# A two-block transformer kernel: the order of the first mixer on four engines is rewritten

## The chip, the cores and the metric

The kernel runs on one core of a Trainium2 chip. The metric is the device time of one execution in microseconds (us). The core's engines run their own instruction streams and meet through semaphores: TensorE (PE; PEld is its weight load), VectorE (DVE), ScalarE (ACT), GpSimd (POOL) and SyncE (SP, which starts the DMAs of weights).

## The reference

Two blocks on 256 tokens of width 1024, all in float32. The change lies in the middle of the first one, its mixer; what it computes:

```python
u = rms_norm(h, ln_mix[i]) @ w_in[i]
hq, hf, hi_, hg, cq, ckv, kr = jnp.split(u, split_at, axis=-1)
log_f = jnp.log(lb + (1.0 - lb) * jax.nn.sigmoid(hf))
k_in = (1.0 - lb) * jax.nn.sigmoid(-hf)
o_hg = hgrn2_chunkwise(hq, log_f, k_in, hi_)          # 4 heads of 128
o_hg = rms_norm(o_hg, hg_out_norm[i]) * jax.nn.silu(hg)

q = rms_norm(cq, q_a_norm[i]) @ w_q_up[i]             # 4 heads, 128 + 64 rope
kv = rms_norm(ckv, kv_a_norm[i]) @ w_kv_up[i]         # keys 128, values 128
o_mla = causal_block_attention(qf, kf, v)             # softmax over 256 tokens
h = h + jnp.concatenate([o_hg, o_mla], axis=-1) @ w_out[i]
```

Before it stand a SwiGLU block (width 2816) and behind it another one, a gated embedding, and the second block: a projection with "forgetting" attention of 16 heads in four groups, and at the end a retrieval of expert rows.

## The kernel before

**Slots.** Every large product is cut into slots of 256 output columns, 2048 weights per partition. SP loads a slot into `ring`, ACT rounds it to `whi` (L947), DVE or POOL makes the rest `wlo` (L326, a split; in the mixer only POOL does it), and PE multiplies three times: high x high (L443), high x low (L444), low x high (L448); in `tokens` these are L465 to L467. A slot has two tiles, t = 0 and 1, a half slot each in `features(n)`; `tokens(n)` has two halves of 128 tokens, and frees both tiles at its end. `whi` holds two slots, so a tile can be rounded once the same half of the slot two earlier is done (`tiles_done`). The mixer's input projection has ten slots, `S_IN` to `S_IN + 9`: forget gates and queries (0 to 3), latents (4, 5), recurrence values (6, 7) and output gates (8, 9). `S_OUT` and the three behind it are the output projection.

**Levels.** The recurrence is computed in eight levels. In `level(n)` PE makes 8 blocks of scores of 128 x 128 into banks 4 and 5 (L607). In `level_read(n)` DVE copies the entries of that level through a mask (L1431); in `widen(n-1)` three DVE products in SBUF (L1445 to L1447) make the operands of level n + 1. A level can begin when the one before it is read and its operands are widened. Operands start with `qf` (L1424). A last level (L698) crosses the two halves; DVE copies it out (L1481) and PE multiplies scores with values (L706 to L708, `hg_out`).

**Latents and heads.** `latent_sums` lets PE sum squares with a stationary matrix of ones, so all partitions hold all 256 sums; ACT takes roots of all of it and DVE the reciprocal (L1456). `q_up`, `k_up`, `v_up` and `swapped` (rotation) are small products in banks 6 and 7 that ACT copies out (L1054). The heads' norm works likewise on 4 x 256 numbers: `hg_sums` (L715), root (L1083), two reciprocals (L1518, L1520).

**Attention.** `attention` makes the scores (L721, L722) and returns `values`, which turns the probabilities (L574, L578), waits for ACT's copy (L1094) and multiplies by the values (L728 to L730). DVE does `softmax` (L1494 to L1501) and `normalise` (L1508 to L1512), ACT the exponentials between them (L1088). `low_x` makes the low part of the input of the next projection (L1297). `keep_busy(n)` issues n matmuls of ones into an unused place; nobody reads them. The second block's attention uses the same functions, with two feature slots and 12 dummies between scores and values.

All orders are written out by hand, one program per engine; each engine executes its own in order.

## Time and profile before

| | us |
|---|---|
| three executions | 1594.4, 1596.62, 1597.06 (median 1596.62) |
| the profiled execution, span | 1596.27, 1594.5 |
| PE busy, DVE, ACT, POOL | 1400.5, 1004.2, 561.5, 710.3 |

Times in rows are from the start of the span. A busy PE is no proof of useful work: dummies count. A row's bracket is the idle time before it and the engine that ended it.

### The profile page before, as it was taken

How to read it: one execution, taken by the hardware profiler on the slowest of the kernel's cores; microseconds unless marked ns; L12 is line 12 of the kernel's file. 1: busy time of each engine (PE TensorE's matmuls, PEld its weight loads, DVE VectorE, ACT ScalarE, POOL GpSimd, SP SyncE). 2: the span in 40 equal slices, each digit the busy share in tenths (PEclk: the TensorE clock that was granted, in tenths of full speed). 3: DMA queues.
4: the chain of work that ended last, by engine and by line, in shares of the span. 5: the costliest groups of instructions: out<-in, count | busy, mean ns of one | idle time of the engine just before them, and what ended most of it. 6: DMA issues, size and time to landing. Idle time of an engine off the chain costs nothing.

```text
span 1594.5 us, 21201 instructions
## 1 busy us (share of the span) xinstructions
PE 1400.5 (88%) x8086; PEld 1071.4 (67%) x8086; DVE 1004.2 (63%) x1792; ACT 561.5 (35%) x947; POOL 710.3 (45%) x443
## 2 busy tenths in 40 slices
PE   8999899998999999989999998777777876877776
PEld 8999899978999998889889883333333332333322
DVE  4887464555778534552543777777777777777654
ACT  4443355424444334554343542222222222222212
POOL 3443437402343534486575485444433443444440
PEclk9999899999999999999999998999998998989998
DMA  5776673303577653243333379999999999999994
GB/s 221 264 263 229 242 251 134 106 27 116 208 263 261 213 180 107 105 135 130 106 107 112 137 289 422 422 421 421 421 421 422 421 421 422 421 422 421 422 421 187
DMA packets 59782, 427.15 MB, mean 268 GB/s; under 512 B 6640, under 2 KB 6960, under 8 KB 8624
## 3 DMA queue, kind: packets, MB, share of 16 engines
q0 software_dynamic: 36864, 268.45, 40.6%
q1 hardware_dynamic: 22176, 156.38, 27.9%
q10 hardware_dynamic: 656, 1.18, 0.2%
q8 instruction: 54, 0.88, 0.2%
q14 instruction: 32, 0.26, 0.0%
HBM read 424.93 MB, written 1.05 MB: 267 GB/s over the span
## 4 chain that ended last, share of the span: by engine, by line
PE 49%; DMA 27%; DVE 13%; ACT 4%; issue 4%; POOL 3%; DVEq 0%; SPq 0%; ACTq 0%; POOLq 0%
DMA rows_x<-in_expert_uv,arena 26%; PE ps L443 8%; PE ps L448 8%; PE ps L444 8%; PE ps L883 5%; PE ps L886 4%; PE ps L520 2%; POOL wlo L326 2%; PE ps L521 2%; PE ps L522 2%; DMA ring<-in_w 1%; DVE arena L1366 1%; DVE arena L1696 1%; ACT whi L947 1%; DVE arena L1512 1%
## 5 line engine op out<-in xcount | busy, mean ns | idle before, releaser
L326 POOL TENSOR_TENSOR wlo<-ring,whi 128x1024 fp32r<-128x1024 f32 x162 | 407.7, 2526 | 497.1 <-ACT whi L947 496.6
L443 PE MATMUL ps<-nh,whi 128*128 128x256 f32 x1440 | 364.3, 290 | 11.3 <-ACT nh L961 6.8
L947 ACT ACTIVATE whi<-ring 128x1024 fp32r<-128x1024 f32 x236 | 244.3, 1055 | 340.2 <-PE ps L448 139.4
L444 PE MATMUL ps<-nh,wlo 128*128 128x256 f32 x1440 | 355.7, 283 | 0.0
L443 PEld LDWEIGHTS ps<-nh,whi 128*128 128x128 f32 x1440 | 276.4, 192 | 17.2 <-issue 8.1
L444 PEld LDWEIGHTS ps<-nh,wlo 128*128 128x128 f32 x1440 | 276.7, 192 | 0.3
L448 PE MATMUL ps<-nl,whi 128*128 128x256 f32 x1440 | 209.2, 285 | 0.1
L448 PEld LDWEIGHTS ps<-nl,whi 128*128 128x128 f32 x1440 | 188.2, 192 | 4.9 <-DVE nl L1304 2.1
L326 DVE TENSOR_TENSOR wlo<-ring,whi 128x1024 fp32r<-128x1024 f32 x74 | 103.8, 1414 | 133.8 <-ACT whi L947 128.6
L1844 POOL DMA_INDIRECT arena<-in_expert_uv,arena x96 | 111.3, 1160 | 141.0 <-PE ps L886 129.4
L1696 DVE CUSTOM_DVE_ANT_0 arena<-arena 128x1024 f32<-128x1024 f32 x96 | 124.7, 1299 | 39.7 <-DMA arena<-in_expert_uv,arena 35.6
L1216 ACT ACTIVATE arena<-arena 128x4 f32<-128x4 f32 (+1 forms) x67 | 13.7, 205 | 348.0 <-DVEq L1698 348.0
L1844 POOL DMA_INDIRECT rows_w<-in_expert_uv,arena x64 | 65.5, 1024 | 114.8 <-PE ps L886 111.7
L1696 DVE CUSTOM_DVE_ANT_0 arena<-rows_w,arena 128x1024 f32<-128x1024 f32 x64 | 78.3, 1224 | 49.2 <-DMA rows_w<-in_expert_uv,arena 48.7
L520 PE MATMUL ps<-gh,whi 128*128 128x256 f32 x352 | 103.8, 295 | 6.2 <-DVE wlo L326 4.5
L883 PE MATMUL ps<-rows_w,silu 128*128 128x512 f32 x96 | 63.0, 744 | 51.7 <-ACT silu L1223 51.7
L1366 DVE SCALAR_TENSOR_TENSOR arena<-arena,vec 128x256 f32<-128x256 f32 x168 | 102.4, 609 | 5.9
L521 PE MATMUL ps<-gh,wlo 128*128 128x256 f32 x352 | 101.1, 287 | 0.0
L522 PE MATMUL ps<-gl,whi 128*128 128x256 f32 x352 | 101.1, 287 | 0.0
L883 PE MATMUL ps<-arena,silu 128*128 128x512 f32 x128 | 69.8, 628 | 29.5 <-ACT silu L1223 29.4
L883 PEld LDWEIGHTS ps<-rows_w,silu 128*128 128x128 f32 x96 | 21.0, 236 | 85.7 <-ACT silu L1223 65.0
L520 PEld LDWEIGHTS ps<-gh,whi 128*128 128x128 f32 x352 | 69.0, 196 | 7.5 <-DVE wlo L326 4.7
(323 smaller groups left out, 2393.6 us busy)
## 6 DMA issues: line engine op xcount, KB each, us to landing
ring<-in_w SPq DMA_DIRECT2D x118, 1024.0 KB, 5.0
arena<-in_wmod SPq DMA_DIRECT2D x24, 1024.0 KB, 5.0
small<-in_small SPq DMA_DIRECT2D x2, 938.5 KB, 7.0
arena<-in_expert_uv,arena POOLq DMA_INDIRECT x96, 26.5
h<-in_x SPq DMA_DIRECT2D x2, 512.0 KB, 5.6
keys<-in_keys SPq DMA_DIRECT2D x1, 1024.0 KB, 7.0
rows_w<-in_expert_uv,arena POOLq DMA_INDIRECT x64, 25.0
small<-in_small SPq DMA_DIRECT2D x1, 939.0 KB, 6.8
```

What stands on the lines that cost most here:

```text
L326: return v.tensor_tensor(wlo[:, tile % TILES, :], ring[:, tile // 2 % RAW, at:at + TILE], whi[:, tile % TILES, :].bitcast(F32), ALU.subtract)
L443: mm(to, hi[:, k, :], nh[:, k, :], start=(k == 0), stop=False)
L444: mm(to, lo[:, k, :], nh[:, k, :], start=False, stop=False)
L448: last = mm(to, hi[:, k, :], nl[:, k, :], start=False, stop=(k == C - 1))
L520: mm(to, hi[:, w, :], gh[:, k, :], start=(k == 0), stop=False)
L521: mm(to, lo[:, w, :], gh[:, k, :], start=False, stop=False)
L522: last = mm(to, hi[:, w, :], gl[:, k, :], start=False, stop=(k == FC - 1))
L883: half = mm(ps[:, acc, :], diagonal(g), rows[:, D:D + 512], start=False, stop=False, skip_group_check=True)
L947: fn(whi[:, tile % TILES, :], ring[:, slot % RAW, at:at + TILE], ACT.Copy).then_inc(S("high_w"), 1)
L1366: own(v.scalar_tensor_tensor(to, wm[:, r, k, :], V("c", k), to, ALU.mult, ALU.add))
L1696: own(v.tensor_tensor_reduce(out=e["junk"], in0=expert_rows(g)[:, 0:D], in1=h2[:, j // PH, :], scale=1.0, scalar=0.0, op0=ALU.mult, op1=AL ...
L1844: nc.gpsimd.indirect_dma_start(g_rows, None, a["expert_uv"], bass.IndirectOffsetOnAxis(ap=unit(j)["index"][:, k:k + 1], axis=0)).then_inc( ...
```

## The change

Four things, in the first mixer only:
- PE: a level stands behind each half slot, from `S_IN + 4` to `S_IN + 7`; the small projections and the scores follow. `features` and `tokens` call `between` after their first half. The dummies of the mixer go.
- The two gate slots move behind the scores, so PE does them while DVE and ACT do the softmax; ACT's rounding of the tiles that they free and its two Silu, too. `attention` is split into `attention`, `turn_probs` and `values`.
- Sums of squares for latents and heads are made with the squares as the stationary operand: each partition holds the sum of one token, and root and reciprocal are taken of 4 and 8 columns (`rsmall`). A product with the identity spreads them over all partitions again; DVE multiplies from PSUM.
- DVE reads the attended values in two halves, and PE no longer waits for that read before `S_OUT`, only for the single high parts of its input.

```diff
             def latent_sums():
                 pe.wait_ge(S("latent_squared"), 2)
-                to = latent(0)
-                mm(to[:, 0, :], ones[:, :], csq[:, 0, :], start=True, stop=False)
-                mm(to[:, 0, :], ones[:, :], csq[:, 1, :], start=False, stop=True)
-                mm(to[:, 1, :], ones[:, :], csq[:, 2, :], start=True, stop=True).then_inc(S("latent_ready"), 1)
+                for b in range(TB):
+                    at = slice(b * P, (b + 1) * P)
+                    mm(ps[:, 6, at], csq[:, 0, at], ones[:, :], start=True, stop=False)
+                    mm(ps[:, 6, at], csq[:, 1, at], ones[:, :], start=False, stop=True)
+                    last = mm(ps[:, 6, T + b * P:T + (b + 1) * P], csq[:, 2, at], ones[:, :], start=True, stop=True)
+                last.then_inc(S("latent_ready"), 1)
+
+            def latent_spread():
+
+                pe.wait_ge(S("latent_inverted"), 1)
+                for b in range(2 * TB):
+                    last = mm(ps[:, 6, b * P:(b + 1) * P], rsmall[:, b:b + 1].to_broadcast([P, P]), ident,
+                              start=True, stop=True)
+                last.then_inc(S("latent_spread"), 1)
...
+                if n <= 2:
+                    pe.wait_ge(S("latent_normed"), n)
...
+            def last_level():
+
+                pe.wait_ge(S("level_operands"), LEVELS + 2)
...
+                last.then_inc(S("level_ready"), 1)
...
+            def hg_out():
+
+                pe.wait_ge(S("scores_built"), 1)
+                pe.wait_ge(S("banks_freed"), S_IN + 8)
...
+            def hg_sums():
+
...
+                for at in range(HH * TB):
+                    hd, b = at // TB, at % TB
+                    last = mm(hg_bank(at), osq[:, hd, b * P:(b + 1) * P], ones[:, :], start=True, stop=True)
+                last.then_inc(S("hg_sums"), 1)
...
+            def hg_spread():
+
+                pe.wait_ge(S("hg_inverted"), 1)
+                for at in range(HH * TB):
+                    last = mm(hg_bank(at), rsmall[:, 2 * TB + at:2 * TB + at + 1].to_broadcast([P, P]), ident,
+                              start=True, stop=True)
+                last.then_inc(S("hg_spread"), 1)
...
+            def sums_and_level():
+                latent_sums()
+                level(4, hqf, hk)
+
+            features(S_IN + 4, between=lambda: level(0, hq, hk))
             level(1, hqf, hk)
-            tokens(S_IN + 6)
-            latent_sums()
-            level(2, hqf, hk)
-            tokens(S_IN + 7)
-            for n in (1, 2, 3, 4):
-                q_up(n)
+            features(S_IN + 5, between=lambda: level(2, hqf, hk))
             level(3, hqf, hk)
-            features(S_IN + 8)
+            tokens(S_IN + 6, between=sums_and_level)
+            latent_spread()
+            level(5, hqf, hk)
+            tokens(S_IN + 7, between=lambda: level(6, hqf, hk))
+            level(7, hqf, hk)
+            q_up(1)
+            q_up(2)
+            last_level()
+            q_up(3)
+            hg_out()
+            q_up(4)
             k_up(5)
             k_up(6)
-            level(4, hqf, hk)
-            features(S_IN + 9)
+            hg_sums()
             v_up(7)
             v_up(8)
-            level(5, hqf, hk)
             swapped(9)
             swapped(10)
-            pe.wait_ge(S("banks_freed"), S_OUT)
-            keep_busy(4, bank=3)
-            level(6, hqf, hk)
+            hg_spread()
             swapped(11)
-            keep_busy(8, bank=3)
-            level(7, hqf, hk)
-            keep_busy(10, bank=3)
-
-            pe.wait_ge(S("level_operands"), LEVELS + 2)
...
-            pe.wait_ge(S("scores_built"), 1)
-            pe.wait_ge(S("banks_freed"), S_OUT)
...
-            def hg_sums():
-
-                pe.wait_ge(S("hg_squared"), 1)
-                for j in range(2):
-                    last = mm(ps[:, 2 + j, :], ones[:, :], osq[:, 2 * j:2 * j + 2, :], start=True, stop=True)
-                last.then_inc(S("hg_sums"), 1)
...
+                last = mm(to[:, P:T], va[:, 1, cols], pt[:, 1024 + hd * P:1024 + (hd + 1) * P], start=False, stop=True)
+                if hd == 1:
+                    last.then_inc(S("attended_first"), 1)
...
             pe.wait_ge(S("rope_done"), 1)
-            rest = attention(0, mla_score, mla_value, m["pr"])
-            hg_sums()
-            keep_busy(44, bank=4)
-            rest()
-
-
-            pe.wait_ge(S("attended_read"), 1)
-            pe.wait_ge(S("hg_gated"), 1)
+            attention(0, mla_score)
+            pe.wait_ge(S("hg_scaled"), 1)
+            features(S_IN + 8)
+            features(S_IN + 9)
+            turn_probs(0, m["pr"])
+            values(0, mla_value)
+
+
             residual(S_OUT, 2, 2)
...
+            act.wait_ge(S("latent_ready"), 1)
+            own(fn(std[:, 0, 0:TB], ps[:, 6, 0:T:P], ACT.Sqrt, bias=eps[:, 0:1], scale=1.0 / (2 * P)))
+            fn(std[:, 0, TB:2 * TB], ps[:, 6, T:2 * T:P], ACT.Sqrt, bias=eps[:, 0:1], scale=1.0 / P
+               ).then_inc(S("latent_copied"), 1)
             values_out(0)
-            act.wait_ge(S("latent_ready"), 1)
-            own(fn(std[:, 0, :], ps[:, 6, 0:T], ACT.Sqrt, bias=eps[:, 0:1], scale=1.0 / (2 * P)))
-            fn(std[:, 1, :], ps[:, 6, T:2 * T], ACT.Sqrt, bias=eps[:, 0:1], scale=1.0 / P).then_inc(S("latent_copied"), 1)
...
             latent_out(3, xr[0:ROPE, 0:2, :], ROPE)
+            act.wait_ge(S("hg_out"), 1)
+            fn(osq[:, :, :].rearrange("p h t -> p (h t)"), ps[:, 0:2, :].rearrange("p b n -> p (b n)"), ACT.Square
+               ).then_inc(S("hg_squared"), 1)
             latent_out(4, xr[0:ROPE, 2:4, :], ROPE)
+            latent_out(5, kn[:, 0:2, :])
+            fn(m["o"], ps[:, 0:2, :].rearrange("p b n -> p (b n)"), ACT.Copy).then_inc(S("hg_copied"), 1)
+            latent_out(6, kn[:, 2:4, :])
+            act.wait_ge(S("hg_sums"), 1)
+            fn(std[:, 0, 2 * TB:2 * TB + HH * TB], ps[:, 2:4, 0:4 * P:P], ACT.Sqrt, bias=eps[:, 0:1], scale=1.0 / P
+               ).then_inc(S("hg_std"), 1)
+            latent_out(7, va[:, 0, :])
+            latent_out(8, va[:, 1, :])
 
             def out_gate(j):
                 product(S_IN + 8 + j)
                 copied(S_IN + 8 + j, fn(hg[:, 2 * j:2 * j + 2, :], pair((S_IN + 8 + j) % BANKS), ACT.Silu))
...
-
-            act.wait_ge(S("hg_out"), 1)
-            fn(osq[:, :, :].rearrange("p h t -> p (h t)"), ps[:, 0:2, :].rearrange("p b n -> p (b n)"), ACT.Square
-               ).then_inc(S("hg_squared"), 1)
-            fn(m["o"], ps[:, 0:2, :].rearrange("p b n -> p (b n)"), ACT.Copy).then_inc(S("hg_copied"), 1)
-            act.wait_ge(S("hg_sums"), 1)
-            fn(ostd[:, :, :].rearrange("p h t -> p (h t)"), ps[:, 2:4, :].rearrange("p b n -> p (b n)"), ACT.Sqrt,
-               bias=eps[:, 0:1], scale=1.0 / P).then_inc(S("hg_std"), 1)
...
             exponentials(0, m["pr"])
+            out_gate(0)
+            out_gate(1)
             turned_probs(0, m["prT"])
 
             act.wait_ge(S("hg_gated"), 1)
             for c in range(C):
                 if c == HH:
+                    act.wait_ge(S("first_read"), 1)
+                if c == HH + 2:
                     act.wait_ge(S("attended_read"), 1)
                 high_x(c)
...
-                own(v.reciprocal(rstd[:, :, :].rearrange("p a t -> p (a t)"), std[:, :, :].rearrange("p a t -> p (a t)")))
+                v.reciprocal(rsmall[:, 0:2 * TB], std[:, 0, 0:2 * TB]).then_inc(S("latent_inverted"), 1)
+
+            def latent_scaled():
+                dve.wait_ge(S("latent_spread"), 1)
                 for k in range(2):
-                    last = v.scalar_tensor_tensor(cqn[:, k, :], cq[:, k, :], V("q_a", k), rstd[:, 0, :], ALU.mult, ALU.mult)
+                    last = v.scalar_tensor_tensor(cqn[:, k, :], cq[:, k, :], V("q_a", k), ps[:, 6, 0:T], ALU.mult, ALU.mult)
                 last.then_inc(S("latent_normed"), 1)
-                v.scalar_tensor_tensor(cqn[:, 2, :], cq[:, 2, :], V("kv_a"), rstd[:, 1, :], ALU.mult, ALU.mult
+                v.scalar_tensor_tensor(cqn[:, 2, :], cq[:, 2, :], V("kv_a"), ps[:, 6, T:2 * T], ALU.mult, ALU.mult
                                        ).then_inc(S("latent_normed"), 1)
...
+            def hg_scaled():
+
+                dve.wait_ge(S("hg_copied"), 1)
+                dve.wait_ge(S("hg_spread"), 1)
+                for hd in range(HH):
+                    ins = v.scalar_tensor_tensor(ho[:, hd, :], ho[:, hd, :], V("hg_norm", hd),
+                                                 ps[:, 2 + hd // 2, hd % 2 * T:(hd % 2 + 1) * T], ALU.mult, ALU.mult)
+                own(ins)
+                dve.sem_inc(S("hg_scaled"), 1)
...
             for n in range(2, LEVELS + 1):
                 level_read(n)
                 widen(n - 1)
+                if n == 3:
+                    latent_inverse()
                 if n == 4:
-
-                    dve.wait_ge(S("latent_copied"), 5)
-                    v.tensor_tensor(rt[0:ROPE, :, :], xr[0:ROPE, :, :], over(cos[:, :], HH + 1), ALU.mult)
...
             dve.wait_ge(S("level_ready"), LEVELS + 2)
             v.tensor_copy(m["sc7"], ps[:, 4, :]).then_inc(S("scores_built"), 1)
+            dve.wait_ge(S("latent_copied"), 5)
+            v.tensor_tensor(rt[0:ROPE, :, :], xr[0:ROPE, :, :], over(cos[:, :], HH + 1), ALU.mult)
+            dve.wait_ge(S("hg_std"), 1)
+            v.reciprocal(rsmall[:, 2 * TB:2 * TB + HH * TB], std[:, 0, 2 * TB:2 * TB + HH * TB]
+                         ).then_inc(S("hg_inverted"), 1)
+            rotate(0)
+            rotate(1)
+            rotate(2)
             v.tensor_tensor(rot[0:ROPE, :, :], rot[0:ROPE, :, :], rt[0:ROPE, :, :], ALU.add).then_inc(S("rope_done"), 1)
+            hg_scaled()
...
             softmax(0, m["pr"], m["st"], float(QK) ** -0.5)
-
-            dve.wait_ge(S("hg_std"), 1)
-            own(v.reciprocal(osq[:, 0:2, :], ostd[:, 0:2, :]))
             normalise(0, m["pr"], m["st"])
-            own(v.reciprocal(osq[:, 2:HH, :], ostd[:, 2:HH, :]))
-            dve.wait_ge(S("hg_copied"), 1)
-            for hd in range(HH):
-                ins = v.scalar_tensor_tensor(ho[:, hd, :], ho[:, hd, :], V("hg_norm", hd), osq[:, hd, :], ALU.mult, ALU.mult)
-            own(ins)
+            dve.wait_ge(S("banks_freed"), S_OUT)
             v.tensor_tensor(mixed[:, 0:HH, :], ho[:, :, :], hg[:, :, :], ALU.mult).then_inc(S("hg_gated"), 1)
+            dve.wait_ge(S("attended_first"), 1)
+            v.tensor_copy(mixed[:, HH:HH + 2, :], pair(5)).then_inc(S("first_read"), 1)
             dve.wait_ge(S("attended"), 1)
-            v.tensor_copy(mixed[:, HH:C, :].rearrange("p h t -> p (h t)"), ps[:, 5:7, :].rearrange("p b n -> p (b n)")
-                          ).then_inc(S("attended_read"), 1)
-
-
-            dve.wait_ge(S("banks_freed"), S_OUT)
+            v.tensor_copy(mixed[:, HH + 2:C, :], pair(6)).then_inc(S("attended_read"), 1)
```

On PE, behind the first half of what was a whole token slot. Before, the sums and level 2 stand behind the whole slot `S_IN + 6` (L465 to L467, then the next slot):

```order
L467 MATMUL ps<-whi,nl 128x256
L620 MATMUL ps<-sq,ones 128x256 [waits latent_squared]
L621 MATMUL ps<-sq,ones 128x256
L622 MATMUL ps<-sq,ones 128x256
L607 MATMUL ps<-arena 128x128 [waits level_read,level_operands]
L607 MATMUL ps<-arena 128x128 x7
L465 MATMUL ps<-whi,nh 128x256 [waits low_pool,banks_freed]
```

Now the sums are six small products and stand with level 4 between the halves of `S_IN + 6`, whose second half follows without a wait of its own (L466 to L468 are `tokens`, L611 is `level`):

```order
L468 MATMUL ps<-whi,nl 128x256
L625 MATMUL ps<-ones,sq 128x128 [waits latent_squared]
L626 MATMUL ps<-ones,sq 128x128
L627 MATMUL ps<-ones,sq 128x128
L625 MATMUL ps<-ones,sq 128x128
L626 MATMUL ps<-ones,sq 128x128
L627 MATMUL ps<-ones,sq 128x128
L611 MATMUL ps<-arena 128x128 [waits level_read,level_operands]
L611 MATMUL ps<-arena 128x128 x7
L466 MATMUL ps<-whi,nh 128x256
```

Two levels more have been done at this place than before. On PE, ahead of the scores, before: levels 6 and 7 with dummies (L483) between them, then the last level and the heads' output:

```order
L483 MATMUL ps<-ones 128x128 x3
L607 MATMUL ps<-arena 128x128 [waits level_read,level_operands]
L607 MATMUL ps<-arena 128x128 x7
L659 MATMUL ps<-arena,con 64x256 [waits rotated]
L483 MATMUL ps<-ones 128x128 x8
L607 MATMUL ps<-arena 128x128 [waits level_read,level_operands]
L607 MATMUL ps<-arena 128x128 x7
L483 MATMUL ps<-ones 128x128 x10
L698 MATMUL ps<-arena 128x128 [waits level_read,level_operands]
L698 MATMUL ps<-arena 128x128 x3
L706 MATMUL ps<-arena 128x128 [waits banks_freed,scores_built]
```

Now, behind the heads' output: `k_up` (L655), head sums (L708), `v_up` (L661), `swapped` (L673), head spread (L715), and the first score (L750):

```order
L655 MATMUL ps<-arena,small 128x256 [waits latent_normed,latent_copied]
L655 MATMUL ps<-arena,small 128x256
L655 MATMUL ps<-arena,small 128x256 [waits latent_copied]
L655 MATMUL ps<-arena,small 128x256
L708 MATMUL ps<-ones,sq 128x128 [waits hg_squared]
L708 MATMUL ps<-ones,sq 128x128 x7
L661 MATMUL ps<-small,arena 128x512 [waits latent_copied] x2
L673 MATMUL ps<-arena,con 64x512 [waits latent_copied] x2
L715 MATMUL ps<-con,rsmall 128x128 [waits hg_inverted]
L715 MATMUL ps<-con,rsmall 128x128 x7
L673 MATMUL ps<-arena,con 64x256 [waits rotated]
L750 MATMUL ps<-arena 128x128 [waits rope_done]
```

The levels are gone from here, and each product waits for a copy of ACT's. On ACT from the last small copies on, now: the exponentials (L1118), the rounding of the next weights (L980), the two Silu (L1114) and the copy of the turned probabilities (L1124); the Silu stood ahead of the copies before:

```order
L1087 ACTIVATE arena<-ps 128x512 [waits latent_ready] x2
L1118 ACT_TABLE_LOAD
L1118 ACTIVATE arena<-arena 128x1536 [waits logits]
L980 ACTIVATE whi<-ring 128x1024 [waits tiles_done,landed1]
L980 ACTIVATE whi<-ring 128x1024 [waits tiles_done]
L1114 ACT_TABLE_LOAD
L1114 ACTIVATE arena<-ps 128x512 [waits tiles_done]
L980 ACTIVATE whi<-ring 128x1024 [waits tiles_done,landed0]
L980 ACTIVATE whi<-ring 128x1024 [waits tiles_done]
L1114 ACTIVATE arena<-ps 128x512 [waits tiles_done]
L1124 ACTIVATE arena<-ps 128x1536 [waits probsT_ready]
```

So four tiles are rounded between the exponentials and that copy, and POOL splits each of them.

## Rows read from the trace of the kernel before

**Rows 1.** Stages: us, then busy (instructions) of PE, PEld, DVE, ACT, POOL; clock, DMA

```profile
293.30:328.80 35.50, 35.26 (x234) 29.59 (x234) 19.80 (x23) 12.99 (x18) 14.51 (x6) 1.00 0.29 99
346.70:367.40 20.70, 16.28 (x129) 14.70 (x128) 20.06 (x20) 6.45 (x8) 0.00 (x0) 1.00 0.00 1
```

**Rows 2.** Timeline of PE, slots and small products: start, us, line, operation

```profile
264.97 1.12 PE L448 MATMUL ps<-nl,whi 128*128 128x256 f32 x8
267.85 1.12 PE L448 MATMUL ps<-nl,whi 128*128 128x256 f32 x8
...
293.29 7.32 PE L632 MATMUL ps<-arena,small 128*128 128x256 f32 x32 [0.40 <-DVE arena L1458]
...
308.18 1.89 PE L641 MATMUL ps<-arena,small 128*128 128x256 f32 x8
309.90 1.95 PE L607 MATMUL ps<-arena 128*128 128x128 f32 x16
311.61 0.36 PE L443 MATMUL ps<-nh,whi 128*128 128x256 f32 x1
```

**Rows 3.** Timeline of PE, from level 6 to the first score

```profile
323.95 2.05 PE L607 MATMUL ps<-arena 128*128 128x128 f32 x16
...
328.83 2.05 PE L607 MATMUL ps<-arena 128*128 128x128 f32 x16 [0.28 <-DVEq L1448]
...
335.66 0.49 PE L706 MATMUL ps<-arena 128*128 128x128 f32 x2 [0.79 <-DVE arena L1481]
...
338.44 0.39 PE L721 MATMUL ps<-arena 128*128 128x128 f32 x2
```

**Rows 4.** Timeline of DVE, a level's masked copy and the last sum of the rotation

```profile
326.04 1.30 DVE L1431 COPY_PREDICATED arena<-lev_mask,ps 128x1024 f32<-128x1024 int32 x1 [1.37 <-PE ps L607]
...
335.52 1.47 DVE L1482 TENSOR_TENSOR arena<-arena 64x1280 f32<-64x1280 f32 x1
```

**Rows 5.** DVE products and POOL's splits; a line view has min/median/max ns

```profile
264.93 2.94 DVE L1424 TENSOR_TENSOR arena<-arena 128x1024 f32<-128x1024 f32 x1 [6.31 <-ACT arena L1037]
...
296.80 2.72 DVE L1446 TENSOR_TENSOR arena<-arena 128x512 f32<-128x512 f32 x1
...
294.12 4.85 POOL L326 TENSOR_TENSOR wlo<-ring,whi 128x1024 fp32r<-128x1024 f32 x2 [4.11 <-ACT whi L947]
...
L1349 DVE TENSOR_TENSOR silu<-silu,ps x22: 672/680/689, 37.1 to 538.2; 128x512 f32<-128x512 f32 x22
```

**Rows 6.** Timeline of DVE and ACT in the first attention

```profile
346.80 0.69 DVE L1494 SCALAR_TENSOR_TENSOR arena<-ps,con 128x512 f32<-128x512 f32 x1 [9.81 <-PE ps L722]
...
352.48 3.35 DVE L1518 RECIPROCAL sq<-sq 128x512 f32<-128x512 f32 x1
...
367.30 2.77 DVE L1297 TENSOR_TENSOR nl<-sq,nh 128x256 fp32r<-128x256 f32 x8
...
352.42 1.48 ACT L1088 ACTIVATE arena<-arena 128x1536 f32<-128x1536 f32 x1 [1.29 <-DVEq L1502]
...
361.46 1.45 ACT L1094 ACTIVATE arena<-ps 128x1536 f32<-128x1536 f32 x1 [7.55 <-PE ps L578]
```

**Rows 7.** Timeline of DVE and ACT in the second attention, first group

```profile
743.77 0.69 DVE L1494 SCALAR_TENSOR_TENSOR arena<-ps,con 128x512 f32<-128x512 f32 x1 [37.08 <-PE ps L778]
...
754.78 3.39 DVE L1512 TENSOR_TENSOR arena<-arena 128x1024 f32<-128x1024 f32 x1
...
759.85 1.45 ACT L1094 ACTIVATE arena<-ps 128x1536 f32<-128x1536 f32 x1 [3.04 <-PE ps L578]
```

**Rows 8.** PE behind two pauses, and a stage (us, busy, clock, DMA) behind the second

```profile
359.89 0.66 PE L574 MATMUL ps<-con,arena 128*128 128x128 f32 x4 [1.39 <-DVEq L1513]
...
739.40 0.98 PE L778 MATMUL ps<-arena 128*128 128x128 f32 x3 [2.68 <-issue]
...
740.00:742.00 2.00, 2.00 (x9) 0.50 0.58 246
```

79 lines of the change are left out of this document (37 added, 42 removed).

## The prediction

> **What bounds the kernel now.** I read the stage table first. The change lies between 268.8 us (first level) and 367.4 us (first output projection), on TensorE (PE), VectorE (DVE) and ScalarE (ACT). Up to 328.8 us PE is busy nearly all the time, so there its own work sets the pace; behind it PE follows a chain: the last levels, the scores, the softmax, the values [rows 1]. In the softmax stretch PE is "busy" for 16.3 of 20.7 us, but most of that is `keep_busy`, matmuls that nobody reads. So there are two reserves: the dummy stretches, and 2 x 5.76 us of real projection work (the gate slots, each two halves of 2.88 us [rows 2]) that now stands ahead of the chain, although nothing needs it before the gated product. Everything behind 367.4 us is the same code in the same order, so what the mixer gains or loses should reach the end as it is.
>
> **The level chain, from rows.** A level costs PE 1.71 us (309.90 to 311.61) [rows 2]. From its start DVE begins reading after 2.09 us (323.95 to 326.04), and the next level may start 2.79 us later (DVE's masked copy and three products of `widen`): 4.88 us from start to start (323.95 to 328.83) [rows 3, 4]. Work between two levels in the new order is 1.71 + 2.88 = 4.59 us. So a half slot nearly, but not quite, covers a level. The first three `widen`s have larger first products (512, 256 and 128 wide); I add 0.1 to 0.5 us, an estimate from the 0.68 us of a 512-wide product [rows 5].
>
> DVE products do not always take their short time. `qf`, 1024 wide, took 2.94 us, one `widen` product of 512 took 2.72 us, while POOL ran `L326` splits; but products of 512 with an operand in PSUM never did so: 22 of them, among the same splits, lie between 672 and 689 ns [rows 5]. I read this as: a DVE product of two SBUF operands that meets a POOL split waits for the end of that split. A token slot ended at 292.89 (PE's next start, 293.29, less its idle 0.40 [rows 2]); POOL ran its two splits from 294.12 to 298.97, back to back: busy from 1.2 to 6.1 us after the end of a token slot [rows 5].
>
> The Trainium skill says the same of the pair of ports in "SBUF — State Buffer", section "SBUF: two separate sides": a two-SBUF-input DVE instruction and a GpSimd instruction exclude each other for a whole instruction, the first one winning. It speaks against this change, which puts `widen` on the path. By a plain sum of DVE's short times the chain would have no such stops and the gain would be larger (second rival below); the rows above already agree with the rule.
>
> **Laying the new order out**, level by level, in the time of the profile before:
> - Level 0 waits for `qf`, which ends at 264.93 + 2.94 = 267.87 [rows 5]: it starts at 267.98, where PE arrives at 265.93 (268.81 less a half). It gains 0.8 us over 268.81 (2.1 us idle, but the second half of the slot is behind it).
> - Level 1: 267.98 + 4.59 = 272.57. Level 2: DVE reads from 274.66; the first product meets the split of the tile freed at 272.57 and loses 0.45: level 2 at 278.35, PE idle 1.2. Level 3 at 283.5 (chain, idle 0.6). Level 4 behind half a token slot and the new sums (12 pieces of 0.107 = 1.28): 289.4, no wait. Level 5 behind the other half and the spread (8 x 0.107 = 0.86): 294.8.
> - Level 6: the token slot ends at 294.0, POOL is busy until about 300.1, and `widen(4)` would begin at 298.15. It waits: level 6 at 301.7 instead of 299.4 (idle 2.3). Level 7 at 306.6, against 328.83 before.
> - The last level: the second token slot ends at 306.3, POOL is busy until 312.4 or 312.5, `widen(6)` begins at 309.95 and its second product gets through after 312.5: last level at 313.85, where two `q_up` (7.32 / 4 = 1.83 each [rows 2]) had covered until 312.0 (idle 1.8).
> - Then PE in its order: last level 0.86, `q_up` 1.83, output of the heads 2.78 (335.66 to 338.44 [rows 3]), `q_up` 1.83, `k_up` 0.86 twice, head sums 16 x 0.107 = 1.71, `v_up` 0.86 twice (`k_up`: 308.18 to 309.90 for two; `v_up` streams as many columns) [rows 2]: 326.3. It waits for ACT, which has three copies, a 1024-wide copy and the small root queued behind the square (about 1 us): 327.3. Two `swapped` 0.9 each (512 columns, as `v_up`), head spread 1.71, `swapped(11)` 0.6, then `rotate(2)` 0.4, the sum of 1.47 and the hand-offs [rows 4]: scores start at 333.6, where they started at 338.44 before [rows 3]. **4.8 us gained.**
>
> Check: between level 7 and the scores lie 27.0 us now, 9.6 before; the levels pay for it with 22.2.
>
> **The softmax stretch.** Before, DVE starts at 346.80 and the low parts of the output projection start at 367.30, 20.5 us later. Two wide reciprocals go (8 numbers instead of 1024; the spread is PE work that stands in the sum above). The first, 3.35 us, holds `normalise` until 355.83, while ACT's exponentials end at 353.90: it costs 1.9 us [rows 6]. The second lies beside PE's transposes and values and costs next to nothing. By itself the removal would shorten the stretch by about 2 us. But the two gate slots free weight tiles, ACT rounds new ones and POOL splits them, under `normalise`. The second attention of this kernel already runs so: its last product takes 3.39 us, and from the start of softmax to the copy of the turned probabilities are 16.1 us (743.77 to 759.85) [rows 7], against 14.7 in the first one (346.80 to 361.46, with the reciprocal in it) [rows 6]. So 1.4 us are lost there instead of 1.9 gained. From there the work is the old one: that copy 1.45 (values from +17.6), values 2.7 (24 pieces of about 0.11), DVE's read of the second two heads 0.7 with hand-offs 0.3 (+21.3; the first two are read under the values), eight low parts 2.77: +24.1. Before they ended at 367.30 + 2.77 = 370.07, which is +23.3 [rows 6]. PE's output slot can start at +20.3, but its first half ends with them. **0.8 us lost**, so 4.0 us remain. The gate slots take 11.5 us of PE, all under the 14.4 us from the start of softmax to its last product (743.77 to 754.78 + 3.39 [rows 7]); their cover is whole.
>
> **The clock.** PE will stand idle from +11.4 (gate slots done) to +14.5 (probabilities), about 3.0 us, where 44 dummies stood. In this trace PE kept the full clock (2.4 GHz) over a pause of 1.39 us [rows 1, 8]; behind the pause of 2.68 us the rows show half of it (0.50, 1.2 GHz) [rows 8]. The second attention fills its pause with 12 dummies and stays at full clock, so it says nothing for this. I expect the clock to fall here, in its short form: the transposes, 1.5 us, take 2.7. Cost 1.2 us. The gaps of 2.1 and 2.3 us in the levels lie between the known cases; I charge nothing for them.
>
> **Sum:** -4.8 + 0.8 + 1.2 = -2.8 us with a fallen clock, -4.0 without; I take -3.4, between the two. The profiled run took 1596.27 us (span 1594.5), 0.35 below the median of 1596.62. The 3.4 us taken from the median: forecast 1593.2 us.
>
> **Rivals.**
> 1. *Forecast*, the layout above, clock held or fallen shortly: 1592.2 to 1594.5. Chance 0.50.
> 2. *Splits miss the products.* Ends of slots and `widen` stand within tenths of a microsecond of each other. If `widen(4)` and `widen(6)` keep their 2.79 us, 2.3 and 1.8 us more come back, and less if only one: -5 to -8, 1588.5 to 1591.5. For it: DVE gets in between two splits (`qf` took 2.94 us, not a whole number of splits). Against: two back-to-back splits leave one gap for three products. Chance 0.15.
> 3. *The clock stays down* through transposes, values and into the output slot. 12 + 24 small pieces and half a slot at twice their time are +1.5, +2.7 and up to +2.9, of which about 3 to 5 us are on the path: gain eaten, 1595.5 to 1598. The four matmul-poor microseconds around ACT's copy speak for it, the 1.39 us case against. Chance 0.22.
> 4. *Slower: DVE is locked out product by product.* For it: the two hits of [rows 5] are each nearly a whole split of 2.4 us. Each further hit on the chain costs up to 2.4 us; three more hits in the seven exposed `widen`s (7.2 us, against the 3 to 4 gained and the 3.2 of the bound) and it is slower by over 0.2%: 1600 to 1604. Against: between the two token slots POOL idles, and only one tile is split per half slot. Chance 0.13.
>
> **Numbers.** 0.2%, 3.2 us, is about what a measurement of this kernel can tell from no change, so "faster" ends at 1593.4. Of case 1 two thirds lie below it (0.33), plus case 2: faster 0.48. Same: the rest of case 1 and nearly all of case 3: 0.38. Slower: case 4 and a little of 3: 0.14. The range must take in cases 1 to 3: 1588.5 to 1598.
>
> **What the profile after would show.** Level starts near 268.0, 272.6, 278.4, 283.5, 289.4, 294.8, 301.7 and 306.6; scores at 333.6; one `widen` product of over 2 us behind level 5 and one behind level 7 with POOL's split over it; the last `normalise` product near 3.4 us; first output slot near 362.4 (just behind 367.3 before); granted clock below 1 around 356 to 360 us. Wrong would make it: level gaps over 6 us in general (case 4), scores before 331 us (case 2), or 0.50 clock lasting beyond 360 us (case 3).

## The result, and the profile after

The changed kernel takes **1603.08 us**, the median of 7 runs (1598.88 to 1607.66), against 1597.06 us for the kernel before beside it (7 runs, 1594.4 to 1606.18). The ratio is 1.0041, 95% interval 1.0021 to 1.0061: slower by 3.4 to 9.7 us. The forecast was 1593.2 us, the range 1588.5 to 1598.0. The profiled execution took 1607.42 us (span 1605.6). One execution of the study, of the first kernel below that holds POOL's splits back, took 2404.94 us at a mean granted clock of 0.75 (0.95 to 0.97 in the others) and is left out.

**The new order stands where the forecast put it.** The timeline of PE, level 0 to level 2 and last level to scores (the number in brackets is PE's idle time ahead of the row, then who ended it):

```profile
268.05 3.41 PE L611 MATMUL ps<-arena 128*128 128x128 f32 x16 [1.82 <-DVE arena L1458]
271.11 0.56 PE L444 MATMUL ps<-nh,whi 128*128 128x256 f32 x1
...
329.71 1.90 PE L673 MATMUL ps<-arena,con 64*64 64x512 f32 x4 [0.78 <-ACT arena L1087]
...
333.52 0.64 PE L673 MATMUL ps<-arena,con 64*64 64x256 f32 x2
336.31 0.49 PE L750 MATMUL ps<-arena 128*128 128x128 f32 x2 [2.14 <-DVE arena L1537]
336.73 0.79 PE L751 MATMUL ps<-arena 64*128 64x128 f32 x2
...
341.79 1.22 PE L750 MATMUL ps<-arena 128*128 128x256 f32 x2
...
349.84 1.22 PE L751 MATMUL ps<-arena 64*128 64x256 f32 x2
350.99 0.58 PE L444 MATMUL ps<-nh,whi 128*128 128x256 f32 x1
...
365.63 0.66 PE L576 MATMUL ps<-con,arena 128*128 128x128 f32 x4 [1.63 <-DVEq L1569]
...
368.70 0.49 PE L757 MATMUL ps<-arena 128*128 128x128 f32 x2 [1.54 <-ACT arena L1124]
```

Levels 1 to 7 start at 274.40, 280.13, 285.29, 291.38, 296.92, 303.65 and 308.55. Level 0 is on time, but from its start to the next product are 3.06 us (268.05 to 271.11), where a level took 1.71 us [rows 2]; the levels behind it stand 1.8 to 2.1 us behind the forecast, the scores 2.7. The scores start at 336.31 instead of 338.44 [rows 3]: 2.1 us gained, not 4.8. And then they take 14.7 us (336.31 to 350.99), where they took about 8.3 before (338.44 to the softmax at 346.70 [rows 3, 1]). The output slot starts at 371.40 us, 4.0 us behind the 367.4 of before [rows 1].

**What is new is the clock.** Stages (busy and count of PE, PEld, DVE, ACT, POOL; granted clock; DMA share and GB/s):

```profile
268.00:272.00 4.00, 3.96 (x20) 3.96 (x21) 0.41 (x1) 0.00 (x0) 2.21 (x1) 0.57 0.69 252
...
330.00:334.20 4.20, 4.17 (x22) 2.31 (x20) 1.37 (x2) 0.87 (x1) 0.00 (x0) 1.00 0.00 0
334.20:336.30 2.10, 0.00 (x0) 0.00 (x0) 1.95 (x3) 0.00 (x0) 0.00 (x0) 1.00 0.00 0
336.00:340.00 4.00, 3.69 (x12) 2.68 (x12) 1.82 (x5) 0.00 (x0) 0.00 (x0) 0.59 0.00 0
340.00:345.00 5.00, 5.00 (x12) 2.61 (x11) 0.00 (x0) 0.00 (x0) 0.00 (x0) 0.50 0.01 3
345.00:350.00 5.00, 5.00 (x10) 2.16 (x9) 0.00 (x0) 0.00 (x0) 0.00 (x0) 0.50 0.00 0
350.00:353.00 3.00, 3.00 (x11) 2.35 (x12) 1.87 (x3) 0.00 (x0) 0.00 (x0) 0.50 0.00 0
353.00:354.00 1.00, 1.00 (x7) 1.00 (x6) 1.00 (x2) 0.00 (x0) 0.00 (x0) 0.59 0.00 0
...
355.00:360.00 5.00, 5.00 (x44) 5.00 (x44) 3.39 (x4) 3.29 (x3) 0.77 (x1) 1.00 0.00 0
```

PE pauses for 2.14 us ahead of the scores. Right behind their first row (336.31 to 336.73) the clock falls from 2.4 to 1.2 GHz; it stays there through the other fifteen rows and nearly three more microseconds, and comes back under the gate slots, near 353.8. The pauses of 1.63 and 1.54 us in the softmax tail, where a fall was forecast, were followed by none. The gate slots, their first pieces at half clock, take 13.0 us from start to end (350.99 to the end of L449 at 364.00), 1.2 more than the 11.8 that they take at full clock in the filled kernel below.

**DVE and POOL do what was forecast.** DVE's products behind levels 5 and 7 and in `normalise`, and POOL's splits:

```profile
300.14 2.07 DVE L1479 TENSOR_TENSOR arena<-arena 128x32 f32<-128x32 f32 x1
...
312.22 2.80 DVE L1480 TENSOR_TENSOR arena<-arena 128x512 f32<-128x512 f32 x1
...
362.10 3.41 DVE L1568 TENSOR_TENSOR arena<-arena 128x1024 f32<-128x1024 f32 x1
...
297.43 4.74 POOL L327 TENSOR_TENSOR wlo<-ring,whi 128x1024 fp32r<-128x1024 f32 x2 [8.81 <-ACT whi L980]
309.80 4.67 POOL L327 TENSOR_TENSOR wlo<-ring,whi 128x1024 fp32r<-128x1024 f32 x2 [7.63 <-ACT whi L980]
359.23 11.81 POOL L327 TENSOR_TENSOR wlo<-ring,whi 128x1024 fp32r<-128x1024 f32 x4 [44.75 <-ACT whi L980]
```

A 32-wide product, 0.2 us of work, ends at 302.21, where POOL's two splits end (302.17).

**Where the time went, by stage of PE** (S_IN: first slot of the mixer's input projections; S_OUT: output slot; "behind": to the start of the second down projection):

| us | S_IN to scores | scores to S_OUT | behind | sum against before |
|---|---|---|---|---|
| before | 100.6 | 29.0 | 164.2 | |
| after | 98.3 | 35.1 | 165.6 | +5.2 |

That is the 3.4 to 9.7 us measured. The profiled span is 11.1 us longer, because it also has a stall far behind the mixer: at the end of the second SwiGLU, PE waits 3.43 us (to 546.45) for a low part from DVE (`wlo`, L327), and runs at a mean clock of 0.54 to 556. That code is unchanged; whether the stall comes with the change is the first question below.

### The profile page after: what moved, and what is told of

Same layout as the page of the kernel before. It is cut to its first block, busy times and chain, and to the rows that moved or that the text cites. A ratio compares the mean times of both kernels' runs of the same rounds, so it can differ in the third digit from the quotient of the medians.

```text
span 1605.6 us, 21019 instructions
## 1 busy us (share of the span) xinstructions
PE 1402.3 (87%) x7996; PEld 1069.7 (67%) x7996; DVE 1003.5 (62%) x1792; ACT 560.1 (35%) x946; POOL 710.1 (44%) x443
## 4 chain that ended last, share of the span: by engine, by line
PE 47%; DMA 27%; DVE 14%; issue 4%; ACT 4%; POOL 3%; DVEq 0%; SPq 0%; ACTq 0%; POOLq 0%
DMA rows_x<-in_expert_uv,arena 26%; PE ps L444 7%; PE ps L449 7%; PE ps L445 7%; PE ps L916 4%; PE ps L919 4%; PE ps L523 3%; PE ps L524 2%; PE ps L525 2%; POOL wlo L327 2%; DVE arena L1400 2%; DMA ring<-in_w 1%; DVE arena L1743 1%; PE ps L611 1%; DVE arena L1568 1%
## 5 line engine op out<-in xcount | busy, mean ns | idle before, releaser
L327 POOL TENSOR_TENSOR wlo<-ring,whi 128x1024 fp32r<-128x1024 f32 x162 | 408.6, 2532 | 507.2 <-ACT whi L980 506.7
L980 ACT ACTIVATE whi<-ring 128x1024 fp32r<-128x1024 f32 x236 | 245.1, 1058 | 349.2 <-PE ps L449 142.8
L449 PE MATMUL ps<-nl,whi 128*128 128x256 f32 x1440 | 210.0, 286 | 0.1
L449 PEld LDWEIGHTS ps<-nl,whi 128*128 128x128 f32 x1440 | 188.6, 192 | 5.4 <-DVE nl L1338 2.1
L327 DVE TENSOR_TENSOR wlo<-ring,whi 128x1024 fp32r<-128x1024 f32 x74 | 104.1, 1418 | 137.4 <-ACT whi L980 131.9
L1743 DVE CUSTOM_DVE_ANT_0 arena<-arena 128x1024 f32<-128x1024 f32 x96 | 124.2, 1293 | 39.2 <-DMA arena<-in_expert_uv,arena 35.1
L916 PE MATMUL ps<-rows_w,silu 128*128 128x512 f32 x96 | 59.3, 704 | 50.8 <-ACT silu L1257 50.8
L916 PE MATMUL ps<-arena,pT 128*128 128x512 f32 x64 | 42.9, 759 | 40.4 <-ACT pT L1257 40.1
```

The costliest lines, as they stand in the source:

```text
L327: return v.tensor_tensor(wlo[:, tile % TILES, :], ring[:, tile // 2 % RAW, at:at + TILE], whi[:, tile % TILES, :].bitcast(F32), ALU.subtract)
L449: last = mm(to, hi[:, k, :], nl[:, k, :], start=False, stop=(k == C - 1))
L916: half = mm(ps[:, acc, :], diagonal(g), rows[:, D:D + 512], start=False, stop=False, skip_group_check=True)
L980: fn(whi[:, tile % TILES, :], ring[:, slot % RAW, at:at + TILE], ACT.Copy).then_inc(S("high_w"), 1)
L1743: own(v.tensor_tensor_reduce(out=e["junk"], in0=expert_rows(g)[:, 0:D], in1=h2[:, j // PH, :], scale=1.0, scalar=0.0, op0=ALU.mult, op1=AL ...
```

## The experiments

Theory A: the order is worth what was forecast, and the loss is the clock, which falls behind pauses of PE of about 2 us that stand in the new order without dummies. Rival B: the stall behind the mixer belongs to the change and is the loss. Rival C: the scores' small products lower the clock by themselves, so no filling helps. Rival D: DVE's stops behind POOL are more than the forecast's. All kernels were timed in five rounds, 6 to 12 executions each. In the first group (the two repeats, all pauses filled, only one filled) the kernel before took 1597.2 us (median of 35 runs), in the second (all filled but one, the dummies taken out of the old order, the two with POOL held back) 1596.89 (27), in the third (two pauses filled, and the last experiment) 1596.6 (23).

**The two kernels again.** No edit.

> The changed kernel once more, unaltered, to see which pauses and half-clock stretches of its first profile come back. Theory A (the clock): the scores again run at half clock behind a pause of about 2.1 us and take over 12 us instead of 8.3; level 0 behind 1.8 us again takes over 3 us. Theory B (the new stall of 3.4 us and the 10 us of half clock at the end of the second SwiGLU, 543 us, belong to the change): that stall comes back too. Rival to B, chance: it is gone or smaller here, and the span is some 5 us shorter. Ratio to before 1.001 to 1.006.

> The kernel before once more, for a second profile and the spread of its time. Theory B: the end of the second SwiGLU is again without a stall over 1.5 us, and half clock appears only in the four places of its first profile. Chance: a stall of 3 us or more with half clock behind it appears there too, and its profile is some 5 us longer. Ratio 0.998 to 1.002.

Measured: the changed kernel 1603.55 us, 1.0032 (1.0013 to 1.0050); the one before 1600.21 us, 1.0011 (0.9990 to 1.0032). PE's timeline, first of the changed kernel's repeat, then of the repeat of before at the end of its second SwiGLU:

```profile
331.59 0.49 PE L750 MATMUL ps<-arena 128*128 128x128 f32 x2 [2.14 <-DVE arena L1537]
...
541.98 0.58 PE L523 MATMUL ps<-gh,whi 128*128 128x256 f32 x1 [3.68 <-DVE wlo L327]
```

```profile
541.47 0.39 PE L520 MATMUL ps<-gh,whi 128*128 128x256 f32 x1 [2.20 <-DVE wlo L326]
```

The half clock in the scores comes again (0.50 from 332 to 349 us). The one at level 0 does not: its stage is 96.8 us instead of 98.3, with the same code and the same order. At the end of the second SwiGLU the changed kernel stalls again (3.68 us). The kernel before stalls there too in its repeat, for 2.20 us and with ten microseconds of half clock behind it, as after the change; stages of the same code there are 75.4 to 82.9 us long over all profiles of this study, and long ones come in either order. B falls as an explanation of the loss: the place scatters without the change.

**The pauses filled.** Dummies ahead of level 0, level 6, the last level, the scores and the turned probabilities:

```diff
+                pe.wait_ge(S("std_ready"), 2)
+                keep_busy(6, bank=4)
+                level(0, hq, hk)
...
+                pe.wait_ge(S("banks_freed"), S_IN + 6)
+                keep_busy(6, bank=3)
+                level(6, hqf, hk)
...
             q_up(2)
+            keep_busy(6, bank=3)
             last_level()
...
             swapped(11)
+            keep_busy(8, bank=4)
...
             features(S_IN + 9)
+            keep_busy(10, bank=4)
             turn_probs(0, m["pr"])
```

> The changed kernel with unread matmuls (6, 6, 6, 8 and 10 of them) in its five pauses of the mixer: ahead of level 0, level 6, the last level, the scores and the turning of the probabilities. Nothing else altered. Theory A: granted clock 1.00 from 268 to 372 us, scores in 8.3 us, S_OUT starting near 363.5 instead of 371.4; 8 us less than the changed kernel, 3 to 4 us less than before (ratio 0.997 to 0.998). Rival (the clock is a symptom and the products wait for something else): scores stay over 12 us although the pauses are filled, ratio stays 1.003 to 1.005.

Measured: 1592.24 us, **0.9962 (0.9944 to 0.9980)**. Timeline of PE at the scores, and the stages of the mixer:

```profile
328.11 2.05 PE L486 MATMUL ps<-ones 128*128 128x128 f32 x16
...
330.32 0.49 PE L762 MATMUL ps<-arena 128*128 128x128 f32 x2 [0.16 <-DVE arena L1550]
...
338.05 0.70 PE L763 MATMUL ps<-arena 64*128 64x256 f32 x2
```

```profile
293.00:326.50 33.50, 31.80 (x207) 25.97 (x207) 15.87 (x17) 10.63 (x15) 7.85 (x4) 1.00 0.19 64
...
330.30:338.70 8.40, 8.38 (x33) 4.76 (x33) 1.53 (x4) 0.00 (x0) 0.00 (x0) 1.00 0.00 0
...
350.00:359.00 9.00, 6.83 (x59) 6.40 (x59) 7.04 (x3) 5.12 (x9) 8.72 (x3) 1.00 0.34 117
```

The clock holds from the first level to the output slot, and the scores take 8.4 us. The levels stand at 263.6, 268.4, 274.1, 279.3, 285.4, 290.9, 297.6 and 302.6; this run reached level 0 4.4 us earlier, and with 4.4 added each is within 0.5 us of the forecast. C falls in its strong form. The stages are 96.8, 28.8 and 165.5: together 2.7 us less than before, where the ratio says 3.2 to 8.9; the table at the end of this section comes back to this.

**Only one pause filled, and all but that one.** First the `keep_busy(8, bank=4)` ahead of the scores alone; then all fillings without it.

> Only the pause ahead of the scores filled (8 unread matmuls). Theory A: the scores take 8.3 us and the gate slots 11.5 again, 7 to 8 us less in the mixer; level 0 still at half clock (1.5 us). The pause ahead of the turned probabilities grows from 1.6 to 3 us and may cost its own half-clock stretch of 1 to 3 us. Ratio to before 0.998 to 1.001. If the earlier pause at level 0 is what lowers the clock for the scores, they stay over 12 us.

> The changed kernel with four of its five pauses filled, the one of 2.1 us ahead of the scores left open. If that pause is what lowers the clock for the scores: scores at half clock again, 12 us or more, and gate slots over 12 us; ratio to before about 1.000. If an earlier pause prepares the fall: scores in 8.3 us, ratio as with all filled, 0.996.

Measured: filled only ahead of the scores 1598.4 us, 1.0004 (0.9983 to 1.0026); all but that one 1602.05 us, 1.0033 (1.0013 to 1.0054). PE's timeline and a stage, of the first and then of the second:

```profile
330.11 0.49 PE L751 MATMUL ps<-arena 128*128 128x128 f32 x2 [0.16 <-DVE arena L1538]
...
333.03 0.48 PE L752 MATMUL ps<-arena 64*128 64x128 f32 x2
333.45 1.22 PE L751 MATMUL ps<-arena 128*128 128x256 f32 x2
```

```profile
336.00:340.00 4.00, 4.00 (x8) 1.74 (x8) 0.00 (x0) 0.00 (x0) 0.00 (x0) 0.50 0.00 0
```

```profile
331.19 0.49 PE L761 MATMUL ps<-arena 128*128 128x128 f32 x2 [2.14 <-DVE arena L1549]
...
332.02 0.68 PE L761 MATMUL ps<-arena 128*128 128x128 f32 x2
```

```profile
332.40:344.60 12.20, 12.20 (x27) 6.30 (x26) 0.30 (x1) 0.00 (x0) 0.00 (x0) 0.50 0.00 0
```

The pause ahead of the scores is enough by itself: with all others filled the scores take 14.3 us (331.19 to 345.44), and the time is that of the unfilled kernel. But filling it alone was not enough: the clock fell all the same, 3.3 us into the scores, which take 12.5 us, with pauses of no more than 0.78 us in the twenty microseconds ahead. The expectation had scores of over 12 us only for the case that a fall at level 0 prepares them, and level 0 ran at full clock here. From the scores back to the last level, this kernel and the one with all pauses filled differ only in the pause ahead of that level (1.68 us, filled to 0.35 there). Further back they differ in the open pauses ahead of levels 0 and 6, and behind the latter the clock had already fallen once in this profile.

**So: the last level and the scores filled**, the pauses of 1.8 and 1.9 us ahead of levels 0 and 6 open.

```diff
             q_up(2)
+            pe.wait_ge(S("banks_freed"), S_IN + 6)
+            keep_busy(6, bank=3)
             last_level()
...
             swapped(11)
+            keep_busy(8, bank=4)
```

> The changed kernel with six dummies of keep_busy ahead of the last level and eight ahead of the scores; the pauses ahead of level 0 (1.8 us) and level 6 (1.9 us) stay open. Theory (the pauses of the last twenty microseconds ahead of the scores are what makes the clock fall in them; with the 1.68 us pause ahead of the last level filled as well, only 0.8 and 0.2 us are left open there): granted clock 1.00 through the scores, which take 8.3 us, and from the first slot of the mixer to the first output projection 126 to 128 us, against 131.4 in the run that filled only ahead of the scores; a short fall near 296 to 300 us, behind level 6's pause, may be there, and a fall at level 0. Time 1593 to 1597. Rival (the scores' own small products make it fall wherever nothing else fills, whatever stands far ahead): half clock inside the scores again, 11 to 12 us, and 1597 to 1600.

Measured: 1596.84 us, 1.0007 (0.9983 to 1.0030). PE at level 6 and at the transposes of the probabilities, then two stages in the scores (332.08 to 340.44 us) and one at the transposes:

```profile
299.41 2.05 PE L611 MATMUL ps<-arena 128*128 128x128 f32 x16 [1.91 <-DVEq L1485]
...
355.06 0.66 PE L576 MATMUL ps<-con,arena 128*128 128x128 f32 x4 [2.86 <-DVEq L1572]
```

```profile
333.00:336.00 3.00, 3.00 (x14) 1.99 (x14) 0.59 (x2) 0.00 (x0) 0.00 (x0) 1.00 0.00 0
336.00:340.00 4.00, 4.00 (x14) 1.97 (x14) 0.00 (x0) 0.00 (x0) 0.00 (x0) 1.00 0.00 0
...
355.00:358.00 3.00, 1.53 (x12) 1.29 (x12) 2.90 (x1) 1.37 (x1) 3.00 (x2) 1.00 0.86 317
```

The scores keep the full clock (8.4 us), and the stages are those of the kernel with all filled (96.8, 28.8, 165.6), as the theory had it. The time is at the upper edge of the expectation, and the profile does not show why it is longer than with all pauses filled.

This profile also has the pause for which the forecast had charged its one fall: with nothing filled ahead of the turned probabilities, PE stands idle for 2.86 us (355.06). The clock holds at 1.00 there, and the transposes take their 1.5 us. So a pause longer than the one ahead of the scores was not followed by a fall.

Two pauses are open here as in the two profiles of the changed kernel and in that with only the scores filled: in one of the four each lowered the clock. The one ahead of level 0 (1.82 or 1.83 us) did so in the first profile of the changed kernel, for 1.5 us; the one ahead of level 6 (1.91 us) in the run filled at the scores, where the level took 3.68 us. So an open pause of 1.8 to 1.9 us is a risk, not a fixed price. That such falls explain the longer time is not shown.

**The dummies taken out of the kernel before**, in its old order:

```diff
-            keep_busy(4, bank=3)
...
-            keep_busy(8, bank=3)
...
-            keep_busy(10, bank=3)
```

> The kernel before without its 22 unread matmuls around levels 6, 7 and the last one; nothing else changed. They hide behind waits, so without the clock the time would be the same. If pauses between small matmuls lower the clock here too, the scores (8.3 us in the kernel before) take 12 us or more in its profile and the ratio is 1.002 to 1.005; if the fall needs what the change brought, ratio 0.999 to 1.001 and scores in 8.3 us.

Measured: 1600.74 us, 1.0024 (1.0008 to 1.0040); S_IN to scores 104.8 us instead of 100.6. PE ahead of level 7, of the last level, and two stages:

```profile
328.87 3.39 PE L607 MATMUL ps<-arena 128*128 128x128 f32 x16 [2.25 <-DVEq L1445]
...
335.08 2.07 PE L695 MATMUL ps<-arena 128*128 128x128 f32 x8 [2.81 <-DVEq L1445]
```

```profile
335.50:341.50 6.00, 5.22 (x24) 4.92 (x24) 2.11 (x3) 0.00 (x0) 0.00 (x0) 0.50 0.01 3
...
342.60:350.00 7.40, 7.40 (x32) 4.35 (x30) 0.00 (x0) 3.22 (x3) 0.00 (x0) 1.00 0.00 0
```

A loss of the same kind without any move of work: 4.2 us for 22 dummies that stood beside waits. The expectation had the fall in the scores, at 12 us or more. It came earlier, at level 7 and at the last level; the second one lasted 6.8 us, and the clock was back before the scores, which take 8.3 us (342.62 to 350.87).

**POOL's splits held back.** Each split of a gate tile waits until a `widen` is done; then also those of the output slot, until the probabilities and the low parts are made. Both keep the fillings at level 0 and the scores; the first also keeps the one ahead of the probabilities.

```diff
-            split(S_IN + 2, S_FFN2)
+            split(S_IN + 2, S_IN + 8)
+            for k, t in enumerate(range(2 * weight_slot(S_IN + 8), 2 * weight_slot(S_OUT))):
+                if k < 3:
+                    pool.wait_ge(S("level_operands"), 7 + k)
+                low(g, pool, t).then_inc(S("low_pool"), 1)
+            split(S_OUT, S_FFN2)
```

and in the second kernel, in place of the last line:

```diff
+            pool.wait_ge(S("probs_ready"), 1)
+            split(S_OUT, S_OUT + 1)
+            pool.wait_ge(S("low_x"), 3 * C)
+            split(S_OUT + 1, S_FFN2)
```

> The changed kernel with the pauses ahead of level 0, the scores and the turned probabilities filled, and POOL's splits of the gate slots' four tiles held back, so that each of the first three runs behind a finished widen (4, 5, 6). If the splits hold up widen(4) and widen(6), as forecast: level 6 starts 4.9 us behind level 5 and not 6.7, the last level 4.9 us behind level 7 and not 7.2, scores 4 us earlier than with the pauses filled alone (level 0 to scores 62.6 us instead of 66.7). Ratio 0.993 to 0.995. Rival: the widen products are slow for another reason (their shapes), then level 5 to 6 stays 6.7 us and the held splits only delay the gate slots.

> As the kernel with the widen splits held, and POOL also holds the splits of the first output slot until the probabilities are ready and those of the second until the low parts are made; no unread matmuls ahead of the turned probabilities. Forecast: normalise's last product 1.2 us instead of 3.4, from the scores' start to S_OUT 3 us less than 28.8, ratio 0.991 to 0.993. Rival: the held splits are late for the output slots, then PE waits inside the output projection by up to 3 us and nothing is left of it.

Measured: the first 1592.58 us (11 executions), 0.9971 (0.9951 to 0.9991), S_IN to scores 92.9 us; the second 1589.66 us (6 executions), **0.9944 (0.9923 to 0.9966)**, with 93.0 and then 25.8 us from the scores to the output slot. DVE, then POOL, behind levels 5 and 7 in the first; then DVE, POOL, PE (the values) and a stage in the softmax of the second:

```profile
299.06 0.18 DVE L1486 TENSOR_TENSOR arena<-arena 128x32 f32<-128x32 f32 x1
...
309.06 0.69 DVE L1487 TENSOR_TENSOR arena<-arena 128x512 f32<-128x512 f32 x1
```

```profile
300.71 2.36 POOL L327 TENSOR_TENSOR wlo<-ring,whi 128x1024 fp32r<-128x1024 f32 x1 [13.16 <-DVEq L1489]
```

```profile
345.65 1.22 DVE L1574 TENSOR_TENSOR arena<-arena 128x1024 f32<-128x1024 f32 x1
349.15 1.32 DVE L1580 TENSOR_TENSOR sq<-arena 128x1024 f32<-128x1024 f32 x1 [2.28 <-ACT arena L1120]
```

```profile
347.00 5.69 POOL L327 TENSOR_TENSOR wlo<-ring,whi 128x1024 fp32r<-128x1024 f32 x2 [35.90 <-DVEq L1575]
```

```profile
350.51 0.49 PE L763 MATMUL ps<-arena 128*128 128x128 f32 x2 [1.72 <-ACT arena L1130]
```

```profile
350.00:355.00 5.00, 4.49 (x38) 4.47 (x39) 2.67 (x6) 3.25 (x9) 2.69 (x1) 1.00 0.24 51
```

The same instructions, moved apart in time: 2.07 us becomes 0.18, 2.80 becomes 0.69, 3.41 becomes 1.22. Level 6 follows level 5 after 4.8 us instead of 6.7. This settles D: the stops exist, cost 3.9 us up to the scores (96.8 to 92.9) and 3.0 behind (28.8 to 25.8), and are those that the forecast's layout had in it.

The measured times show less than these stages. Both ratios missed their expectations (0.993 to 0.995, and 0.991 to 0.993). Against the kernel with all pauses filled (0.9962), the first is not faster at all (0.9971), and the second is 2.9 us faster (0.9944), with intervals of about 3 us on either side of each. The Trainium skill states the cause in "SBUF — State Buffer", section "SBUF: two separate sides": an exclusive lock, held for a whole instruction, between GpSimd and a DVE instruction with two SBUF inputs. The rows agree: the 32-wide product took 2.07 us up to the end of the splits, and 0.18 us where no split ran.

**The same with the last pause filled** (`keep_busy(8, bank=4)` ahead of the values).

> The kernel that holds POOL's splits back to the ends of the products (all of them), with eight dummies more in the pause of 1.7 us ahead of the values, where it kept the full clock without them. Theory (a single pause of 1.7 us behind several microseconds of transposes and projections costs no clock): the same time as that kernel within 0.2%, 1588 to 1591.5, from the scores to the first output projection 25.8 us, granted clock 1.00 there in both. Rival (that pause now and then lowers the clock into the output slot, and the one profile did not meet it): up to 3 us less than that kernel, 1586 to 1588. Either way faster than the kernel before by 0.3 to 0.7%.

Measured: 1587.03 us, **0.9944 (0.9924 to 0.9965)**: the same ratio, and the same stages (92.9 and 25.9 us, clock 1.00). The single pause of 1.72 us costs nothing there. Both versions beat the kernel before, by 5.4 us or more.

**All stages together.** The table gives the sum of the three stages (the way from S_IN to the second down projection) against the 293.8 us of the first profile of the kernel before, whose repeat is at +0.5, and the 95% interval of the measured time against the kernel before.

| kernel | stages | measured |
|---|---|---|
| changed, first profile | +5.2 | 3.4 to 9.7 |
| changed, repeat | +3.7 | 2.1 to 8.0 |
| all filled | -2.7 | -8.9 to -3.2 |
| filled at the scores alone | +3.2 | -2.7 to 4.2 |
| filled but at the scores | +4.0 | 2.1 to 8.6 |
| filled at the last level and the scores | -2.7 | -2.7 to 4.8 |
| old order, dummies out | +4.5 | 1.3 to 6.4 |
| POOL held at the gate tiles | -6.0 | -7.8 to -1.4 |
| POOL held, all | -9.3 | -12.3 to -5.4 |
| the same, values filled | -9.2 | -12.1 to -5.6 |

The stages lie inside the interval or at its edge in all but one row, that of all filled, where they miss it by 0.5 us. The two kernels with the same stages, all filled and two filled, were measured at -6.1 and +1.1 us. Their mean, -2.5, is what the stages give, so the 0.4% of gain measured for the first may be partly luck.

## Why the prediction was wrong, point by point

- **The level chain and its layout: right.** With the clock held, every level is within 0.5 us of its forecast time, with the two long products where they were named. The way from level 7 to the scores takes 27.8 us instead of 27.0. The gain up to the scores is 3.8 us (100.6 to 96.8) for a forecast 4.8: mechanism right, size 1.0 off.
- **The softmax stretch: right.** 0.8 us lost was forecast. Measured in the filled kernel: the output slot 0.2 us nearer, and 1.3 us more behind it: 1.1 us lost. The last product took 3.41 us for 3.4 forecast, and the cover of the gate slots was whole. The 1.3 us behind the output slot's start belong to the new order: that stage is 165.5 to 166.1 us long in its nine profiles, and 164.2 to 164.7 in the three of the old one.
- **The clock: the step that failed.** "The gaps of 2.1 and 2.3 us in the levels lie between the known cases; I charge nothing for them." Those two pauses, measured as 1.8 and 1.9 us, lowered the clock in one of four profiles each. The loss came from a third, of 2.14 us ahead of the scores: it lowered the clock in three of three profiles that left it open. This pause was itself in the layout (`swapped(11)`, then `rotate(2)`, the sum and the hand-offs), but was never named as a pause of PE. The forecast put its one fall ahead of the turned probabilities, for 1.2 us; that pause came out as 1.63 us instead of 3.0, since the gate slots had started late and slow, and the clock held. Where it came out at 2.86 us (two pauses filled), the clock held too, so this term of 1.2 us was seen in no run.
- **The price of a fall: too low in the sum.** 1.2 us was priced for the transposes alone. In the scores it costs 6.4 us (14.7 for 8.3), since the clock does not come back in them: 17 us at 1.2 GHz, from 336.8 to 353.8. The gate slots' 1.2 us more lie under the softmax and cost nothing. Rival 3 had this effect at another place, at 3 to 5 us; the case "slower" was given to rival 4, whose mechanism did not come.
- **Sum in the runs:** -3.8 (up to the scores) + 1.1 (softmax tail) = -2.7 us with the clock held. With the fall in the scores (+6.4) it is +3.7, which is what the stages of the repeat give (96.8 + 35.1 + 165.6, less 293.8 of before); the first profile has 1.5 more at level 0: +5.2.

## What to carry to other kernels

Dummy matmuls beside a chain are not a free reserve: before they go, list every pause that PE will have in the new order, also those that follow from a handful of instructions, and price each of about 2 us and more as a risk, by the work that follows it, at half clock. Sixteen short rows of score products cost 6.4 us here, and 36 dummies in five pauses turned 0.3 to 0.4% of loss into 0.4% of gain by the measured time, 0.2% by the stages. Then read the clock behind every pause in the profile: a pause's length alone did not tell whether it would fall. Where DVE and POOL meet on a chain, hold POOL's work back to the end of DVE's products: it took 6.8 us out of the mixer's stages, of which the measured times show 2.9 (0.9962 to 0.9944).
